# Two-layer hybrid decoder trunk on one core: g and b steps, a moved sum, a shared affine and another last unit

## What is computed

```python
def reference(x, c, w_in, conv_w, mix_norm_g, w_out, w_mod, b_mod, ln1_g, ln1_b, w_ff1, w_ff2, ln2_g, ln2_b):
    cond = jax.nn.silu(c)
    for l in range(DEPTH):                       # DEPTH = 2
        mod = cond @ w_mod[l] + b_mod[l]
        sh1, sc1, g1, sh2, sc2, g2 = jnp.split(mod[:, None, :], 6, axis=-1)
        u = x * (1.0 + sc1) + sh1
        q, k, v, gate_b, gate_c, h_in = jnp.split(u @ w_in[l], SPLIT_POINTS, axis=-1)
        attn = _dilated_mixture(_rotary(heads(q)), _rotary(heads(k)), heads(v))
        conv = gate_b * _causal_short_conv(gate_c * h_in, conv_w[l])
        mixed = _group_rms_norm(jnp.concatenate([attn, conv], axis=-1), mix_norm_g[l])
        x = _layer_norm(ALPHA * x + (1.0 + g1) * (mixed @ w_out[l]), ln1_g[l], ln1_b[l])
        u = x * (1.0 + sc2) + sh2
        ff = jnp.square(jax.nn.relu(u @ w_ff1[l])) @ w_ff2[l]      # 2048 -> 8192 -> 2048
        x = _layer_norm(ALPHA * x + (1.0 + g2) * ff, ln2_g[l], ln2_b[l])
    return x
```

## Time and profile before

| | |
|---|---|
| median of the runs | 2389.97 us |
| profiled execution | 2390.11 us, its span 2388.4 us |
| PE, share of the span | 95% |
| DVE | 72% |
| ACT | 47% |
| POOL | 10% |
| mean granted clock of PE | 0.983 |

### The profile page before, as it was taken

The page is one execution under the profiler, slowest core; times in us unless marked ns, Lnnn a source line. Parts: engine busy times, 40 slices in busy tenths (PEclk is TensorE's granted clock), DMA queues, the critical chain, the costliest instruction groups (busy, mean ns, idle before and its releaser), DMA issues.

```text
span 2388.4 us, 30251 instructions
## 1 busy us (share of the span) xinstructions
PE 2270.1 (95%) x10384; PEld 1881.5 (79%) x10384; DVE 1728.5 (72%) x1913; ACT 1115.9 (47%) x1424; POOL 227.3 (10%) x400
## 2 busy tenths in 40 slices
PE   3689999989999999999998999999999999999997
PEld 2577888778888888888877888887888888888885
DVE  6898888868777767667878877877766555555566
ACT  2235543356435435435454554435643543543543
POOL 2211111110101101000010100101000000000000
PEclk9789999989999999999999999999999999999998
DMA  9987988958888888887965777886677666666563
GB/s 354 390 289 283 306 324 316 325 211 283 285 283 293 287 276 298 276 276 268 321 242 184 267 262 257 287 293 220 224 237 242 206 213 215 213 205 193 177 228 123
DMA packets 174733, 623.14 MB, mean 261 GB/s; under 512 B 19728, under 2 KB 20496, under 8 KB 174096
## 3 DMA queue, kind: packets, MB, share of 16 engines
q1 hardware_dynamic: 114128, 407.50, 49.8%
q0 software_dynamic: 55296, 201.35, 24.8%
q10 hardware_dynamic: 5184, 12.59, 1.6%
HBM read 619.27 MB, written 2.10 MB: 260 GB/s over the span
## 4 chain that ended last, share of the span: by engine, by line
PE 84%; DVE 8%; DMA 3%; issue 3%; ACT 2%; ACTq 0%; SPq 0%; DVEq 0%; POOLq 0%
PE bank L1249 25%; PE bank L1251 25%; PE bank L1250 25%; DVE mod_acc L770 3%; PE bank L1350 2%; PE bank L1325 2%; DVE w_lo L755 1%; DMA raw<-w_out_dram 1%; DMA Z<-w_mod_dram 1%; ACT w_hi L455 1%; PE bank L1263 1%; PE bank L1264 1%; PE bank L1265 1%; ACT utmp L496 0%; DVE xt L877 0%
## 5 line engine op out<-in xcount | busy, mean ns | idle before, releaser
L755 DVE TENSOR_TENSOR w_lo<-raw,w_hi 128x1024 fp32r<-128x1024 f32 x768 | 937.8, 1224 | 563.7 <-ACT w_hi L455 561.7
L455 ACT ACTIVATE w_hi<-raw 128x1024 fp32r<-128x1024 f32 x768 | 812.4, 1059 | 1129.2 <-PE bank L1251 988.4
L1249 PE MATMUL bank<-w_hi,u_hi 128*128 128x512 f32 x1744 | 695.3, 399 | 0.3 <-DVE u_lo L813 0.3
L1251 PE MATMUL bank<-w_lo,u_hi 128*128 128x512 f32 x1744 | 682.0, 391 | 0.0
L1250 PE MATMUL bank<-w_hi,u_lo 128*128 128x512 f32 x1744 | 681.5, 391 | 0.0
L1249 PE MATMUL bank<-w_hi,m_hi 128*128 128x512 f32 x1216 | 476.9, 392 | 2.8 <-DVE m_lo L813 2.6
L1251 PE MATMUL bank<-w_lo,m_hi 128*128 128x512 f32 x1216 | 474.5, 390 | 0.0
L1250 PE MATMUL bank<-w_hi,m_lo 128*128 128x512 f32 x1216 | 474.3, 390 | 0.0
L770 DVE SCALAR_TENSOR_TENSOR mod_acc<-mod_raw,cond,mod_acc 128x1024 f32<-128x1024 f32 x300 | 383.7, 1279 | 0.6 <-DMA mod_raw<-w_mod_dram 0.6
L1251 PEld LDWEIGHTS bank<-w_lo,u_hi 128*128 128x128 f32 x1744 | 328.9, 189 | 70.0
L1249 PEld LDWEIGHTS bank<-w_hi,u_hi 128*128 128x128 f32 x1744 | 329.5, 189 | 68.6 <-issue 1.4
(11 more groups left out here) (128 smaller groups left out, 1116.5 us busy)
## 6 DMA issues: line engine op xcount, KB each, us to landing
raw<-w_ff_dram SPq DMA_DIRECT2D x512, 512.0 KB, 4.2
mod_raw<-w_mod_dram POOLq DMA_DIRECT2D x320, 512.0 KB, 5.4
raw<-w_in_dram SPq DMA_DIRECT2D x192, 512.0 KB, 5.2
Z<-w_mod_dram POOLq DMA_DIRECT2D x64, 512.0 KB, 9.1
raw<-w_out_dram SPq DMA_DIRECT2D x64, 512.0 KB, 5.7
gate<-b_rows_dram ACTq DMA_DIRECT2D x4, 1024.0 KB, 4.9
Z<-ln_g_dram ACTq DMA_DIRECT2D x16, 256.0 KB, 6.3
Z<-ln_b_dram ACTq DMA_DIRECT2D x16, 256.0 KB, 7.0
```

The source lines that it names most:

```text
L455: nc.scalar.activation(w_hi[:, j % AHEAD, :], raw[:, j % RAW, :], ACT.Copy).then_inc(hi_ready, 1)
L755: nc.vector.tensor_tensor(w_lo[:, j % AHEAD, :], raw[:, j % RAW, :], w_hi[:, j % AHEAD, :].bitcast(F32), ALU.subtract).then_inc(lo_ready, 1)
L1249: nc.tensor.matmul(o, hi[:, k, tok], wh, start=(k == 0), stop=False)
L1251: ins = nc.tensor.matmul(o, hi[:, k, tok], wl, start=False, stop=(k == KC - 1))
```

## The change

- `gain` leaves the first units. It takes its quarter from `GAIN_ORDER`. In the mixer of layer 1 the four gains are at positions 9, 11, 13 and 17 of that part, in the MLPs at 9, 12, 14 and 17. ACT waits for them before it writes `QT`, `KT` and `V` in layer 1; it clears `acc` one unit later (w = 3). The q transposes of layer 1 move from position 10 to 14.
- The mod steps that were in unit 1 of those parts (in the last MLP, units 1 and 2) go to later units. Slab 9's sum moves from position 124 to 127.
- In a last unit position 7 comes, on PE, after the first half group of tile 1, on DVE after `last_tile` of tile 0; `modulation` comes after it.
- In jobs 4 to 7 of a fill DVE does the affine of columns 2 and 3 (new `affine`), and ACT, after it, that of columns 0 and 1.
- In the very last unit PE does all 8 half groups of tile 0, then all 8 of tile 1. The weights of groups 0 to 3 are put into `u_hi` and `u_lo`, which are free by then.
- The ending: DVE does (x - mean) * g for four quarters (`centre`), the root, and then * root + b (`scaled`), each in one operation; ACT normalises nothing.

```diff
@@ def mod_positions():
-    ff0 = sorted([8 * w + j for w in range(1, FF_UNITS - 1) for j in (1, 3, 4, 6)]
-                 + [8 * w + 7 for w in (1, 2, 3, 9, 10, 11, 17, 18)])
-    mixer1 = sorted([8 * u + j for u in range(1, 15) for j in (0, 2, 4, 6) if u + j > 1]
-                    + [8 * u + 1 for u in (1, 2, 3, 4, 9, 10, 11, 12, 13)])
-    ff1 = sorted([8 * w + 4 for w in range(1, 25)] + [8 * w + 1 for w in range(1, 9)])
+    ff0 = sorted([8 * w + j for w in range(2, FF_UNITS - 1) for j in (1, 3, 4, 6)]
+                 + [8 * w + 7 for w in (2, 3, 8, 9, 10, 11, 16, 17, 18, 19, 24, 25)])
+    mixer1 = sorted([8 * u + j for u in range(2, 15) for j in (0, 2, 4, 6)]
+                    + [8 * u + 1 for u in range(2, 14)])
+    ff1 = sorted([8 * w + 4 for w in range(3, 25)] + [8 * w + 1 for w in range(3, 13)])
...
-Q_AT = [[22, 34], [10, 34]]
+Q_AT = [[22, 34], [14, 34]]
...
-RED_NOT_BEFORE = {16: MIXER_AT[1] + 8, 17: MIXER_AT[1] + 12}
+RED_NOT_BEFORE = {9: MIXER_AT[0] + 8 * U_MIX - 1, 16: MIXER_AT[1] + 8, 17: MIXER_AT[1] + 12}
...
+FINAL = DEPTH * U_LAYER - 1
+GAIN_ORDER = {1: (0, 1, 2, 3), 2: (2, 0, 1, 3), 3: (0, 1, 2, 3)}
+MIX_GAIN_AT = (9, 11, 13, 17)
+FF_GAIN_AT = (8 + 1, 8 + 4, 8 + 6, 16 + 1)
...
+        def weights(w, ex, unit, j):
+
+            if unit == FINAL and j < EARLY:
+                return ex[:].rearrange("p k n -> p (k n)")[:, j * GW:(j + 1) * GW]
+            return w[:, j % AHEAD, :]
@@ ACT, prepare
-                    act.wait_ge(pair_used, 8 * unit + (j - AHEAD + 1))
+                    act.wait_ge(pair_used, 8 * unit + (j - AHEAD + 1 if unit < FINAL or j < EARLY else j - GROUPS + 1))
@@ ACT, fill_job
-                for c in range(4):
+                if i >= 4:
+
+                    act.wait_ge(aff_ready, 4 * (fill - 1) + i - 3)
+                for c in range(4 if i < 4 else 2):
@@ DVE
+            def affine(fill, i):
+
+                t, s = NORM_ORDER[i]
+                job, n = JOB[("fill", fill)] + i, fill_split(fill, i)
+                wait_job(dve, job)
+                dve.wait_ge(split_ready, n - 1)
+                for c in range(2, 4):
+                    k = 4 * s + c
+                    ins = nc.vector.tensor_scalar(utmp[:, n % 2, c * P:(c + 1) * P], tb[job % 2][:, c * P:(c + 1) * P],
+                                                  u_scale[:, k:k + 1], u_shift[:, k:k + 1], ALU.mult, ALU.add)
+                ins.then_inc(aff_ready, 1)
...
+            def centre(t):
+
+                for s in range(4):
+                    dve.wait_ge(gb_in[s], 32 * 2 * DEPTH)
+                    sl = xt[:, t, s * NCOL:(s + 1) * NCOL]
+                    nc.vector.scalar_tensor_tensor(out=sl, in0=sl, scalar=mv[:, t, 0:1], in1=lngb[:, s, 0, :],
+                                                   op0=ALU.subtract, op1=ALU.mult)
+
+            def scaled(t):
+
+                for s in range(4):
+                    sl = xt[:, t, s * NCOL:(s + 1) * NCOL]
+                    nc.vector.scalar_tensor_tensor(out=sl, in0=sl, scalar=rst[:, t:t + 1], in1=lngb[:, s, 1, :],
+                                                   op0=ALU.mult, op1=ALU.add).then_inc(x_ready, 1)
@@ DVE, last_unit
-                for j in range(EARLY, GROUPS):
+                for j in range(EARLY, GROUPS - 1):
                     side(j)
+                last_tile(fill, unit, alpha, 0)
+                side(GROUPS - 1)
                 modulation(fill)
-                last_tile(fill, unit, alpha, 0)
                 last_root(fill, 0)
@@ DVE, first_unit
                 for j in range(GROUPS):
+                    if j < 4:
+                        affine(fill, 4 + j)
                     ahead(unit, j)
                     if j < 4:
                         fill_low(fill, 4 + j)
-                    else:
-                        gain(fill, j - 4)
                     side(j)
@@ DVE, the end
-            last_tile(fill, unit, 1.0, 0)
-            last_root(fill, 0)
-            gain(fill, 0, (0,))
-            last_tile(fill, unit, 1.0, 1)
...
+            for t in range(T):
+                last_tile(2 * DEPTH, FINAL, 1.0, t)
+                centre(t)
+                sync(root(norm_index(2 * DEPTH, t), slice(t, t + 1)))
+                scaled(t)
@@ PE, last_unit
-                for j in range(EARLY):
+                both = 0 if unit == FINAL else EARLY
+                for j in range(both):
...
+                for j in range(both, GROUPS):
+                    half(unit, j, pacc[par][1], 1, hi, lo).then_inc(pair_used, 1)
+                    if j == EARLY:
+                        side(GROUPS - 1)
```

65 lines of the change are left out of this document (31 added, 34 removed).

## The result

| | before | changed |
|---|---|---|
| median of the runs | 2389.97 us | 2373.73 us |
| lowest to highest | 2387.24 to 2394.49 | 2370.97 to 2376.64 |
| ratio to before | 1 | 0.993 [0.9915, 0.9945] |
| profiled execution | 2390.11 us | 2372.73 us |
| its span | 2388.4 us | 2371.1 us |

The change makes the kernel faster, by 0.55 to 0.85%. The forecast was 2371.6 us; the median is 2.1 above it and inside the range. A kernel with the same code, run again in a later group (e12), gave 2373.03. One run of the kernel before, in the group of e5 to e8, took 12433 us in a slow state; the ratios leave it out.

A forecast was written before the change was run, and what follows sets the result against it. TensorE, busy 95% of the span, was taken as the bound, leaving its waits and half-rate stretches. Savings of 6.3 + 7.1 + 3.0 - 0.4 + 2.35 = 18.4 us gave 2371.6 us, range 2366 to 2379.5.

The forecast's parts named there:

- Part 1: Layer 0's mixer to ff transition: slab 9's sum behind tile 1's first half group saves 6.3 us, bounds 3.3 to 7.7.
- what is late next: Step at the moved slab sum: w_lo of half groups 6 and 7 arrives late, costing 1.4 us with overhead.
- Part 2: Layer 1 after its first unit: moving the g and b gains removes PE's q transpose wait, 7.1 us less, bounds 0 to 7.5.
- rival (b): Layer 1's q transposes: the wait only moves to position 14, at most all 7.1 us return, 2378.7 us; chance 0.07.
- Part 3: First units: sharing the affine between ACT and DVE saves 1.0 us, three times; bounds 0 to 1.95.
- a round becomes about 2.75: First units: one ACT round of w_hi, affines and u_hi falls from 3.0 to about 2.75 us.
- The clock: Three gaps before first units and a new one at the end may flip PE's rate, 2 us each; taken as unchanged.
- Part 4: Last unit and end: tail from 17.5 to 12.9 us, minus a 2.25 us PE wait; net 2.35 us less.
- The modulation behind the variance: Two transitions without a sum: three modulation steps go behind the variance on DVE, charged +0.2 us twice.
- (c): Layer 1's mixer, units 2 to 13: DVE becomes the bound, 2 us over per unit gives 2395.6 us; chance 0.05.
- (a): Clock turns unfavourable: layer 1's gap, the last unit's new gap and part 1's rate loss give 2377.5 us; chance 0.14.
- the first four cases: Forecast, clock turning bad, smaller edges, and q wait only moving: counted as faster, below 2382.8 us, together given 0.89.

The follow-up runs named there:

- e12: The changed kernel run once more with the same code, nothing changed: 2373.03 us, ratio 0.9932.
- e1: Changed kernel with slab 9's sum back at position 124, between half groups 4 and 5 of tile 0: 2379.42 us, ratio 0.9959.
- e5: Changed kernel with the last unit in its old order (both tiles per group in groups 0 to 3), fused ending kept: 2373.19 us, ratio 0.9922.
- e8: Changed kernel with DVE's affine of the next job queued ahead of u_lo of this job: 2372.16 us, ratio 0.9923.
- e3: Kernel before with only layer 1's q transposes moved from position 10 to 14, gains still in the first unit: 2384.84 us, ratio 0.9979.
- e9: Changed kernel with layer 1's q transposes back at position 10, gains still spread: 2373.62 us, ratio 0.9929.
- e4: Changed kernel with all four affines of jobs 4 to 7 on ACT again, none on DVE: 2378.11 us, ratio 0.9954.
- e2: Changed kernel with the gains back in the first units, old mod positions and layer 1's q transposes at position 10: 2381.52 us, ratio 0.9966.
- e10: Changed kernel with the mod steps at their old positions in layer 1's mixer, gains still spread: 2375.21 us, ratio 0.9935.
- e7: Changed kernel with the mixers' eight g and b loads issued in four pairs at positions 104, 107, 110 and 113: 2372.65 us, ratio 0.9932.
- e6: Changed kernel with the residual of the unit before the last put behind the last unit's w_lo's of groups 4 to 7: 2369.30 us, ratio 0.9903.
- e11: Changed kernel with residual behind the last unit's w_lo's, paired g and b loads, and DVE's next affine ahead of u_lo: 2366.01 us, ratio 0.9904.

## Why the prediction was right, and where it was not

**Part 1: right as a mechanism; the size can't be right to better than a microsecond.** 5.8 against 6.3 in this pair of traces; e1 gives all of it back. The two waits for w_lo are where the DVE rows put them: the step "what is late next" kept this term from being 7.7. But it read one execution. The same code in e12 has none of the two waits and takes 1.8 us less, and the wait for the sum that the term starts from, 2.87 us, was 1.54 in e3. The prediction gave bounds for half rate and for an early w_lo, and none for a DVE that comes earlier in the kernel before. That the number came so close is in part luck.

**Part 2: right in size, and for the stated reason.** 7.18 against 7.1. The forecast said that PE "waits 5.44 us for just that" and priced the half rate behind it from its rows. It followed DVE's queue in the times of before, and the changed kernel is 8.9 us ahead there (8.2 at the gap ahead of its first unit, 1241.86 in the earlier trace rows against 1233.65, and 0.7 in that unit). The rotation was put at about 1272 and came at 1263.03 + 8.9 = 1271.9; gate sum 17 was put at 1290.1 and came at 1289.5; PE was put at 1291.4 and came at 1292.0. The margin was 1.3 in the forecast and is 2.5, so rival (b) did not happen. One thing was in the same numbers and was not drawn from them: with gate sum 16 done at 1278.9, PE at position 10 (1291.4 - 10.9 = 1280.5) would not have waited either. e9 shows just that. What e3 shows is the case of moving the consumer alone: the wait goes to w_lo, the next in DVE's queue.

**Part 3: the mechanism right, the term too large.** The bank waits and the second transition give 0.67 to 0.75 us each (e4), not 1.0. The step that failed is "a round becomes about 2.75": it is 2.95. DVE's pair was put at 0.6 and "partly under ACT's w_hi". It takes 0.72, starts only behind u_lo, and is then in series with ACT's pair, for which ACT waits 0.53 us in each round. e8 puts the pair ahead of u_lo and gets 2.3 to 2.4. That the three sum to 3.0 all the same is the clock of the first transition, and so luck. (The term's upper bound of 1.95 does not follow from its rows either: both waits gone is 0.86 + 0.99 = 1.85.)

**The clock: taken as unchanged, not so.** Before, half rate followed two of the three gaps of 2.6 us; in the changed kernel's trace one. In the second trace of the same code all three were. Over all 14 traces of this case there are 42 such gaps, and half rate followed 24 of them. A half-rate case costs about 0.9 us net (19.1 against 18.1), and not the 2 us of the forecast: some eight steps of 0.43 in place of 0.23 are 1.6 us, and the w_lo wait of 0.41 that a full-rate PE runs into goes away (with it two steps of 0.80 and 0.31, some 0.65 over full rate). The Trainium skill, TensorE: Matmul & The Clock Gate, Part 1, says that the gate's window is free-running; that equal gaps in equal code end both ways is in line with it, but no run here separates it from other causes.

**Part 4: the wait right, what follows it left out, and the tail too long.** The wait was forecast at 2.25 us and measured at 2.13. By the account, 39.02 - 37.39 = 5.64 - 2.13 - 1.88, another 1.9 us went behind it. Of these 0.3 come with the wait in every trace that has it (PE's pass of the last unit is 21.53 us without a wait, and 23.97 to 23.99 with a wait of 2.14 and full rate behind it), and 1.6 are the half rate (25.54 to 25.59 with it). The half rate stood only among the bounds; it came in e2, e9, e10 and e12 as well, and did not come in e1, e4, e7 and e8. With five of nine it is as likely as not, so the sum could be right only to about 0.8 us either way here, and half of it should have stood in the likeliest value. (The lower bound of 0.3 is 2.35 - 1.9 = 0.45 by its own figures.) The tail was forecast as 12.9 and is 11.85. DVE's share was right to 0.2 us: 2.55 for the residual and the variance, 3.4 for centring and root (a pitch of 0.66 and not 0.61), 2.74 for scaling, end at 2368.39. The error is in the store: 4.0 forecast, 2.7 measured. The packets of the four stores of 256 KB run from 2367.3 to 2370.2, and the span ends 0.8 us after the last of them; before, it ended 1.4 after it. The longest of the four took 2.4 us from issue to landing; before, the last one took 3.2. What makes the difference is open, as no run touched the stores.

**The modulation behind the variance:** charged 0.2 twice, measured 0.07 at the second and third turn (3.63 to 3.70, from the turn's start to the first unit) and 0 at the first. On DVE the reciprocal of the root starts 0.57 us after the variance in place of 0.42, so most of the three steps lies in the time in which DVE waited for ScalarE's root.

**Not foreseen:** 1.2 us in layer 1's mixer, of the burst of eight loads. The forecast had looked for what the change moves, and the change moves nothing there; the price varied over the traces from 0.2 to 1.4 us.

**Rivals.** (c), DVE as the bound of the mixer, did not happen: in units 2 to 13 of layer 1 PE waits for DVE nowhere longer than in the kernel before but for that one w_lo. The mod steps were free, and e10 shows that leaving them in unit 1 would have cost about 0.9. (a) cannot be told from the forecast by one trace: some of its half rate came (the last unit) and some of it did not. One sum there is off: the first four cases have 0.60 + 0.14 + 0.12 + 0.07 = 0.93, and not 0.89.

The errors against the sum: 0.5 lost in part 1, 0.1 won in part 2, 0.9 lost in part 3's size, 0.9 won by the clock in the same rows, 0.7 lost in part 4, 1.2 by the burst, and 1.4 won in the rest (0.4 of it the modulation that was charged, the other 1.0 in no row of the forecast). They leave the span 1.1 us short of 18.4. Errors of 3.3 us to the one side and 2.4 to the other met in a sum that was off by 1. The other 1.0 us up to the median is that the profiled execution, 2372.73, lay under the median of its runs, 2373.73.

## What to carry to other kernels

- When PE waits for an engine, write down that engine's queue around the wait and move what nobody needs soon (here the gains) behind what PE needs. Moving the consumer instead won 3.2 of 7.2 us, since the queue stayed long and the next thing in it, w_lo, became late.
- A pass that is made faster needs its inputs faster. Tile by tile the last unit wanted a w_lo per half group, and six residual operations ahead of them cost 2.4 us with the wait and, in five of nine traces, 1.6 more of half rate; with them put behind, the same order won 4.0 (e6).
- To share one step between two engines helps only if the second engine's part can run while the first is busy with something else; in series it gave 0.05 us a round, and 0.6 once it was queued earlier (e8). Loads issued by an engine that also computes cost less here when issued in pairs beside its work (e7, e11).
- A term read from one trace has the spread of that place over executions. Part 1's stretch lay between 11.6 and 14.2 us in traces in which nothing about it had been changed; a second trace of the kernel before would have shown that its wait is not fixed.

## What the runs showed of the hardware

- Gaps of 2.59 to 2.67 us in PE's stream, in the same code at the same place, were followed by either level: in all 14 traces by full rate 18 times and by half rate 24 times. After the wait of 2.13 us in the last unit it was 4 and 5. Where half rate came it began with the first step or up to some five matmuls later (at the fourth matmul in e12's first gap). What decides it is not settled by these runs.
- Of eight DMA issues in a row on ACT's queue the first took 0.34 us and the others 0.5 to 2.4 (1.14, 2.42 and 1.30 for the last three), with ACT at no other work for 6.9 us; in pairs (e7) the first took 0.33 and the second 0.45 to 0.92.
- Two 128x128 affines out of PSUM take 0.72 us on DVE and 0.81 on ACT, where four take 1.49 on ACT.
